# Projections and attention of a two-block layer put into one stage: gate tiles last, first maxima of the scores computed between the last projection tiles

## The reference, cut to what matters

```python
p = u @ w_in[l]                                   # 1024 -> 2816 columns: q, k, v, za, a, g, zc
q, k, v = qk_heads(p, qn_w, kn_w)                 # RMS norm per head
q, k = rope_2d(q, angles), rope_2d(k, angles)
k_all = jnp.concatenate([k_c, k], axis=1)         # 256 + 2048 = 2304 keys
s = jnp.einsum('bqkgd,bskd->bkgqs', qblk, k).astype(jnp.float32) * scale
pr = jax.nn.softmax(s, axis=-1)
attn = attend_blocked(q, k_all, v_all) * jax.nn.silu(za)
u = a * jax.nn.sigmoid(g)                         # conformer branch
y = conv(u, conv_w)                               # depthwise, 31 taps over tokens, 512 channels
conv = (silu(layer_norm(y)) @ w_pw + b_pw) * jax.nn.silu(zc)
out = jnp.concatenate([attn, conv], axis=-1) @ w_out
```

## Time and profile before

| | |
|---|---|
| time, median of 3 runs | 2630.91 us (2628.75 to 2632.73) |
| time of the profiled execution | 2630.01 us |
| its span | 2627.9 us |
| PE busy | 2469.1 us (94%) |
| DVE busy | 1678.9 us (64%) |
| ACT busy | 1008.6 us (38%) |
| POOL busy | 696.8 us (27%) |
| projections, first to last matmul | 1026.84 to 1557.99 us |
| first piece of attention | 1590.24 us |
| first score | 1604.54 us |
| first matmul of the stage output | 2368.58 us |

### The profile page before, as it was taken

One profiled execution on the slowest core, in us unless ns is written; L12 is line 12 of the kernel. 1 busy time (PEld: TensorE's weight loads), 2 busy tenths in 40 slices (PEclk: granted clock), 3 DMA queues, 4 the chain that ended last, 5 costly groups with the idle time before them and its releaser, 6 DMA issues. The chain is left out here.

```text
span 2627.9 us, 33255 instructions
## 1 busy us (share of the span) xinstructions
PE 2469.1 (94%) x11265; PEld 1700.2 (65%) x11265; DVE 1678.9 (64%) x2746; ACT 1008.6 (38%) x1766; POOL 696.8 (27%) x313
## 2 busy tenths in 40 slices
PE   4999999999999998999999977999999999978997
PEld 1577777777777776777777753445455545536776
DVE  3235655564555550979997985777777777774664
ACT  4144453444345331322222124555444544452222
POOL 0244212101101100102000004677656556640000
PEclk8999999999999999999999986999999999998999
DMA  8965878489477746488767554111111111004334
GB/s 309 332 213 166 281 258 284 154 272 341 146 269 270 270 177 237 161 311 300 249 208 257 196 172 105 53 49 46 29 31 31 28 30 27 25 25 170 132 140 152
DMA packets 225145, 453.62 MB, mean 173 GB/s; under 512 B 23957, under 2 KB 82571, under 8 KB 224756
## 3 DMA queue, kind: packets, MB, share of 16 engines
q1 hardware_dynamic: 195000, 353.14, 39.8%
q10 hardware_dynamic: 30012, 98.77, 10.9%
HBM read 328.86 MB, written 109.35 MB: 167 GB/s over the span
## 5 line engine op out<-in xcount | busy, mean ns | idle before, releaser
L2140 DVE TENSOR_REDUCE att_mx<-att_bank_m 128x1 f32<-128x512 f32 (+1 forms) x640 | 365.1, 629 | 128.3 <-PE att_bank_m L1949 128.3
L2089 ACT ACTIVATE att_p_f<-att_bank_s 128x512 f32<-128x512 f32 x576 | 312.3, 599 | 281.7 <-PE att_bank_s L1990 273.5
L1934 POOL TENSOR_TENSOR att_den<-att_den,att_p_f 128x1024 f32<-128x1024 f32 x160 | 379.4, 2371 | 40.1 <-ACT att_p_f L2089 24.8
L1637 DVE SCALAR_TENSOR_TENSOR proj_conv_acc<-proj_conv_in,proj_conv_w,proj_conv_acc 128x512 f32<-128x512 f32 (+1 forms) x480 | 337.4, 772 | 0.0
L574 PE MATMUL gla_bank_g<-mid_a_hi,mid_w_hi 128*128 128x512 f32 x768 | 311.8, 406 | 1.8 <-POOL mid_w_lo L527 1.1
L574 PE MATMUL gla_bank_g<-mid_a_hi,mid_w_lo 128*128 128x512 f32 x768 | 302.0, 393 | 0.0
L574 PE MATMUL gla_bank_g<-mid_a_lo,mid_w_hi 128*128 128x512 f32 x768 | 301.4, 392 | 0.0
L1964 PE MATMUL att_bank_o<-att_p_f,att_v 128*64 128x512 f32 x1152 | 269.4, 603 | 0.0
L574 PEld LDWEIGHTS gla_bank_g<-mid_a_hi,mid_w_hi 128*128 128x128 f32 x768 | 145.4, 189 | 47.9 <-issue 18.7
L1964 PEld LDWEIGHTS att_bank_o<-att_p_f,att_v 128*64 128x64 f32 x1152 | 74.6, 137 | 145.2 <-issue 103.8
L574 PEld LDWEIGHTS gla_bank_g<-mid_a_hi,mid_w_lo 128*128 128x128 f32 x768 | 145.2, 189 | 31.4
(11 more groups left out here) (406 smaller groups left out, 4747.3 us busy)
## 6 DMA issues: line engine op xcount, KB each, us to landing
mid_w_hi<-scratch_w_hi SPq DMA_DIRECT2D x100, 512.0 KB, 4.6
mid_w_lo<-scratch_w_lo SPq DMA_DIRECT2D x100, 512.0 KB, 6.2
mid_w_hi<-scratch_w_hi ACTq DMA_DIRECT2D x84, 512.0 KB, 3.8
mid_w_lo<-scratch_w_lo ACTq DMA_DIRECT2D x84, 512.0 KB, 4.9
scratch_w_hi<-mid_w_hi SPq DMA_DIRECT2D x54, 512.0 KB, 6.2
scratch_w_lo<-mid_w_lo SPq DMA_DIRECT2D x54, 512.0 KB, 7.1
mod_wslab<-in_ada_w SPq DMA_DIRECT2D x6, 2048.0 KB, 17.9
first_w_raw<-in_w_in SPq DMA_DIRECT2D x22, 512.0 KB, 7.9
```

Of the source, the lines that this page charges most:

```text
L1637: dve.scalar_tensor_tensor(acc, src, conv_w[:, c, k:k + 1], acc, ALU.mult, ALU.add).then_inc(taps, 1)
L1934: pool.tensor_tensor(den[s][:], pair(0) if j == 1 else den[s][:], pair(j), ALU.add).then_inc(den_pool, 1)
L2089: act.activation(p_f[:, kt, :], S[kt % SBANKS][:], ACT.Exp, scale=float(HD) ** -0.5).then_inc(p_done, 1)
L2140: dve.reduce_max(mx[:, qt, n:n + 1], M[p % MBANKS][:, 0:min(TB, KEYS - TB * n)], AX_X).then_inc(mx_read, 1)
```

## The change

The two stages become one function with one block and one barrier in front. `attention` no longer runs its own block; it returns for each engine the pieces of work that the projections call at given turns, and a `rest` that follows the last turn. Its semaphores are taken when the projections begin, and its tiles are given fixed places at which they can stand beside those of the projections that are still in use. The semaphores of both are cleared once, behind attention, where attention's alone were.

- The turns are in three rounds, listed by `ROUNDS`: block 0; convolution and heads of block 1, convolution of block 2, gates of block 1; heads of block 2, convolution and heads of block 3, and last all sixteen gates of blocks 2 and 3. `TAPS_OF_TURN` gives the taps of each of the 88 turns (0 in the last), `STORE_TAPS` when they are stored. Keys are the first of the five heads to be turned (`HEADS`).
- In round 2 SP loads the keys of group 0 in four parts (`KEYS_AT`, j = 14, 18, 22, 27), the first queries (j = 14), and the values in five parts of full rows (j = 30 to 34). ACT rounds the first queries and keys at j = 28 and 29. DVE makes the keys' remainders in four parts (j = 30 to 33) in place of POOL.
- PE makes four of the 20 pieces of step 0 after each of the last five turns; DVE reduces them at the start of its turns j = 32 to 35, the last four and the column in the last one.
- Keys of group 1 are loaded in step 0 once the last projection tile is done; they are rounded after kt 9 of step 0, their remainders made by DVE after kt 11 and 14.
- In the last step the squares and the ACT work of the layer norm stand one key tile earlier, and in the tail of DVE `add_o` and the swishes swap places.

The core of the diff:

```diff
-def projections(nc, d, keep):
+def projections_and_attention(nc, d, keep):
...
+    HEADS = (4, 0, 1, 2, 3)
+    CONV, HEAD, GATE = range(0, 8), range(8, 14), range(14, NW)
+    ROUNDS = (((0, CONV), (0, HEAD), (0, GATE)), ((1, CONV), (1, HEAD), (2, CONV), (1, GATE)),
+              ((2, HEAD), (3, CONV), (3, HEAD), (2, GATE), (3, GATE)))
...
+    KEYS_AT = {14: slice(0, 768), 18: slice(768, 1280), 22: slice(1280, 1792), 27: slice(1792, KEYS)}
...
+    TAPS_OF_TURN = [0, 0, 0, 0, 7, 7, 6, 5, 7, 6, 9, 4, 12, 12, 2, 7, 4, 5, 1, 3, 3, 4, 5, 7, 7, 1, 7, 7, 7, 7, 9, 8, 6, 4, 6, 5, 3, 7, 6, 5, 3, 3, 4, 4,
+                    4, 7, 8, 8, 8, 8, 8, 8, 8, 8, 7, 7, 7, 9, 4, 8, 7, 6, 4, 3, 4, 4, 6, 9, 10, 9, 10, 9, 4, 8, 7, 7, 3, 3, 3, 4, 4, 5, 5, 6, 5, 5, 4, 0]
...
+    made = dict(keep, S=(BQ, BS, G[0]), M=(BN, BX, BY, BV), O=G[1], tiles=UP + NB * NW, proj=proj, q_stored=q_stored, z_stored=z_stored,
+                    conv_stored=conv_stored)
+    begin = attention(nc, d, made, ctx)
...
+                    if r == 2 and j >= GATES_LAST + 4:
+                        first_maxima(4 * (j - GATES_LAST - 4))
+                    if t == NB * NW - 1:
+                        first_maxima(16)
+                        first_column()
...
+                    if r == 2 and j == GATES_LAST + 3:
+                        split_first_q()
+                    if r == 2 and GATES_LAST + 2 <= j < GATES_LAST + 6:
+                        rest_of_k(0, j - GATES_LAST - 2)
+                    next_taps(sum(TAPS_OF_TURN[:t]), TAPS_OF_TURN[t])
+                rest()
...
-                for g in range(NKV):
-                    pool.wait_ge(k_hi_done, UP + g + 1)
-                    pool.tensor_tensor(k_b[g][0:HD, :], k_raw[g][0:HD, :], k_a[g][0:HD, :].bitcast(F32), ALU.subtract).then_inc(k_lo_done, 1)
...
+        def rest_of_k(g, n):
+            part = slice(KEYS // K_PARTS[g] * n, KEYS // K_PARTS[g] * (n + 1))
+            dve.wait_ge(k_hi_done, UP + g + 1)
+            dve.tensor_tensor(k_b[g][0:HD, part], k_raw[g][0:HD, part], k_a[g][0:HD, part].bitcast(F32), ALU.subtract).then_inc(k_lo_done, 1)
```

1596 lines of the change are left out of this document (843 added, 753 removed).

## The result

The changed kernel takes 2609.65 us (median of 4, 2607.06 to 2614.77), the kernel before 2631.09 (median of 4, 2628.75 to 2632.73). The ratio is 0.992 with an interval of 0.9907 to 0.9933. It is faster, by 21 us or 0.8%; 2587 had been forecast, and the time lies 10.65 us above the range of 2579 to 2599.

The account below looks back on a forecast made before the run. PE, busy 94% of the 2627.9 us span, was taken as the bound, with time lost at the stage boundary. Terms -46.55 + 4.4 + 2.7 + 3.6 - 6.4 + 1.0 - 2.5 + 0.8 = -43.0 gave 2587 us, range 2579 to 2599.

Parts of the forecast that it names:

- The gap between the stages: From the last projection tile to the first attention score: 4.4 us in place of 46.55.
- I take 0 for turns 0 to 82: Projections in the new order: PE sets the pace, DVE catches up by turn 60, so no time lost.
- I take nothing for them: Loads of keys, first queries and values: requested several turns of 5.44 us before use, so no cost.
- The last five turns, +3.6 us: PE waits for late DVE reductions in turns 84 to 86: +3.6 us, between 1 and 7; pieces add +2.7.
- -6.4 us: Step 0 of attention at the full clock takes 16.3 us to the column of step 1, where it took 22.74.
- rival 4: DVE's remainders collide with POOL in step 0, up to 4 us each; price +0 to +3 us; chance 0.03.
- Rival 1: Remainders and reductions make DVE late in turn 84, or the clock falls behind the last tile; about 2592; chance 0.12.
- Rival 3: Keys of group 1 land late in step 0 and hold up ACT; +1 to +5 us, about 2590; chance 0.07.
- Rival 2: Head chains run short of time in turns 46 to 60 and stall PE; +4 to +6, about 2592; chance 0.12.
- the slower side: The new order makes DVE the bound in the projections; time above 2631 us; chance 0.04.
- The last step: Squares and sums one key tile earlier shorten ACT's and PE's waits: -2.5 us, between 0 and -4.
- The boundaries: A longer clear of semaphores behind attention: +0.8 us, between 0 and 2.

Follow-up runs that it names:

- experiment 4: Changed kernel with all 20 pieces and reductions of step 0 put behind the last tile, as before the change; 2607.34 us, ratio 0.9909.
- experiment 1: Changed kernel with each group of four first-maxima reductions done in the turn of its pieces, ahead of that turn's taps; 2605.73 us, ratio 0.9909.
- experiment 5: Changed kernel with eight taps moved from turns 82 to 86 into turns 76 to 80; 2603.54 us, one run.
- experiment 9: Changed kernel with three buffers for the finished gates in place of two; 2607.97 us, one run.
- experiment 10: Changed kernel with maxima reduced ahead of taps, eight taps moved earlier, twelve unread matmuls behind the last tile and a third gate buffer; 2592.89 us, ratio 0.9845.
- experiment 2: Changed kernel with twelve matmuls nobody reads (filler): eight behind the last four pieces, four behind the transposes of the maxima; 2602.75 us, ratio 0.9916.
- experiment 6: Changed kernel with twelve unread matmuls, and the first remainder of group 1's keys moved from kt 11 to behind the column at kt 14; 2602.22 us, one run.
- experiment 12: Changed kernel with the last step and tail put back as before the change; 2608.61 us, one run.
- experiment 11: Changed kernel with twelve more unused semaphores in the joined stage, each raised at its start and cleared at its end; 2614.12 us, one run.

## Why the prediction was wrong

**The gap between the stages: right.** 4.64 us against 4.4 forecast, 41.9 us gone against 42.15.

**"I take 0 for turns 0 to 82": right for PE, wrong for what follows.** PE lost nothing there (experiment 4: 531.33 against 531.15 us; the longest wait is 0.6 us). But the step went through DVE's work and left SP's queue out. The sentence "I take nothing for them", on the requests of keys, queries and values, is the one that failed: they, and the eight swaps of each head, stand on SP ahead of the gate stores. The store that DVE then waited for was issued 9 us behind its gate and took 8.1 us to land.

**The last five turns, +3.6 us: the mechanism right, the size off.** 3.6 us of waits were forecast from a start of the reductions 7.2 us behind tile 83. It was 11.1, and PE waited 6.0 + 0.4 + 0.6 + 0.7 = 7.7 us. The sum also held nothing for the clock: the pieces and tile 85 behind the wait took some 2.5 us more than others of their kind. With 2.7 us of pieces, which was right, the turns cost 14.7 us against 6.3; the last 1.8 us I have not traced one by one, but a tile between pieces takes 5.7 us and not 5.4. Experiments 1, 4, 5, 9 and 10 show the main part by taking the lateness away in different ways.

**Step 0: the step "-6.4 us" failed.** The forecast called the clock a rival at 0.12 and took the four pieces and the transposes for work enough. They were not. The filler gives back 5.05 us (experiment 2). Moving the first remainder away gives 2.4 us more (experiment 6); its contention with POOL, rival 4, can be at most 3.34 - 1.34 = 2.0 of them, and no run takes it alone. What then remains is 17.09 us for the 17.3 forecast, but in a kernel with one remainder less ahead of the column, so that the agreement is in part luck. Rival 1 in both its halves came true, and rival 4 with it; the forecast had weighed them as alternatives. Its "at twice 1.4 us they would take up to 4 us each" is a slip: twice 1.4 is 2.8, and 2.92 was measured. Rival 3 did not come in the changed kernel, where ACT rounds the keys of group 1 without a wait; it waited 2.5 us only where the filler had made step 0 faster. Rival 2 and the slower side did not come.

**The last step.** -2.5 forecast; 2.2 to 2.5 by experiment 12. Yet the whole stretch from mz of step 1 to the tail's end is only 0.5 us shorter than before, and the rows of the clock say where the rest went. Step 2 takes 25.2 us from mz to mz with its stretch at the lower level, 23.6 before and in the kernels that have none there, so 1.6 us; the stretch in the last step costs 44.3 - 43.1 = 1.2 us. Of these 2.8 us the ledger shows 2.0, since mz of step 1 comes 0.9 us closer to its scores than before and so starts the column later. The kernel before had the upper level throughout. The forecast put the clock behind step 0 at nothing. Why it falls in these two places is open: the same waits of 1.2, 0.3 and 0.6 us stand in the last step of the changed kernel, where it fell, and of the filler kernel, where it did not.

**The boundaries.** +0.8 forecast; +0.9 ahead of the projections and +1.4 behind attention. The first grows with the semaphores (experiment 11), the second is open.

**Chance.** The profiled execution of the changed kernel came 5.5 us later out of the stages that nobody changed. Its own median is 1.7 us lower than it. The sum of the misses is 8.4 (turns) + 7.3 (step 0) + 2.0 (steps 1 to 31 and tail) + 1.5 (boundaries) + 5.5 (chance) + 0.2 (gap) - 0.3 (output) = 24.6 us, and 2587.0 + 24.6 = 2611.6, the profiled execution's 2611.34. Without the 5.5 us it would still lie above the range.

The clock, by the Trainium skill's page "TensorE: Matmul & The Clock Gate" (Part 1): a gap of idle PE brings the lower level. The rows agree for the wait of 6 us. In step 0 the clock fell at about 1585 though no single wait exceeded 2.4 us; a spell of short waits was enough there, and twelve matmuls in it kept the clock. The contention of DVE and POOL is as the Trainium skill's page "SBUF — State Buffer", section "Who interferes with whom", has it: 3.34 us beside POOL's additions, 1.34 without.
